# Loading x in four quarters, and splitting the first two weight units ahead of the first chunks of x

## The reference

```
f1 = swiglu(rms_norm(x, ffn1_pre_g), ffn1_w_gate, ffn1_w_up, ffn1_w_down)   # 1024 -> 2816 -> 1024
x  = x + 0.5 * rms_norm(f1, ffn1_post_g)
x  = x + rms_norm(token_mixer(rms_norm(x, mix_pre_g), ...), mix_post_g)      # 8 + 8 heads of 64
x  = x + 0.5 * rms_norm(swiglu(rms_norm(x, ffn2_pre_g), ...), ffn2_post_g)
gate = sigmoid(rms_norm(x, ple_pre_g) @ w_ple_gate)
x  = x + rms_norm(gate * (p @ w_ple_proj), ple_post_g)
```

## Time and profile before

| | |
|---|---|
| median of 3 runs | 1197.67 us (1196.76, 1197.9, 1197.67) |
| profiled execution, first to last instruction | 1196.8 us (no other time of it is shown) |
| TensorE matmuls busy | 1150.8 us, 96% |
| VectorE busy | 635.6 us, 53% |
| ScalarE busy | 510.1 us, 43% |
| GpSimd busy | 64.9 us, 5% |
| bytes read | 94.44 MB, 81 GB/s over the span |

### The profile page before, as it was taken

How to read it: one execution, slowest core, us unless ns; L and a number is a source line. 1 busy time by engine, 2 the same in 40 slices (tenths; PEclk the granted TensorE clock), 3 DMA queues, 4 the chain that set the end, 5 groups by cost and what they waited for, 6 DMA issues and landing times.

```text
span 1196.8 us, 15572 instructions
## 1 busy us (share of the span) xinstructions
PE 1150.8 (96%) x5066; PEld 938.9 (78%) x5066; DVE 635.6 (53%) x1007; ACT 510.1 (43%) x909; POOL 64.9 (5%) x68
## 2 busy tenths in 40 slices
PE   7999999999997999999999998799999999999897
PEld 6888888888885877888788776588888888888675
DVE  6454454542226865655556658945454454333745
ACT  5433333332224455646556653443333334333536
POOL 5000000000001300000000003400000000000120
PEclk9999999999998988998888899899999999999999
DMA  5233333322222311211111013133333334444001
GB/s 177 89 88 105 96 96 96 98 97 96 96 97 71 80 27 53 54 45 43 35 31 39 27 45 81 48 100 97 96 88 105 96 107 126 139 151 135 1 18 71
DMA packets 99011, 97.02 MB, mean 81 GB/s; under 512 B 7136, under 2 KB 82976, under 8 KB 98976
## 3 DMA queue, kind: packets, MB, share of 16 engines
q1 hardware_dynamic: 98976, 96.56, 27.1%
HBM read 94.44 MB, written 2.10 MB: 81 GB/s over the span
## 4 chain that ended last, share of the span: by engine, by line
PE 88%; DVE 7%; ACT 3%; issue 1%; DMA 0%; DVEq 0%; SPq 0%; ACTq 0%
PE bank L1106 28%; PE bank L1108 27%; PE bank L1107 27%; PE bank L1345 2%; DVE xT L788 2%; PE bank L1323 1%; DVE w_r L746 1%; DVE scratch L1052 1%; DVE xg L772 1%; PE bank L1311 1%; DVE acc L766 1%; ACT xg L459 1%; PE bank L1126 1%; PE bank L1376 1%; DVE scratch L1069 0%
## 5 line engine op out<-in xcount | busy, mean ns | idle before, releaser
L746 DVE TENSOR_TENSOR w_r<-w_raw,w_r 128x512 fp32r<-128x512 f32 x332 | 231.6, 706 | 386.1 <-ACT w_r L427 385.8
L427 ACT ACTIVATE w_r<-w_raw 128x512 fp32r<-128x512 f32 x332 | 206.2, 629 | 448.0 <-PE bank L1108 447.0
L1106 PE MATMUL bank<-xg,w_r 128*128 128x512 f32 x890 | 355.8, 400 | 4.6 <-DVE xg L772 4.6
L1107 PE MATMUL bank<-xg,w_r 128*128 128x512 f32 x890 | 351.5, 395 | 0.0
L1108 PE MATMUL bank<-xg,w_r 128*128 128x512 f32 x890 | 351.0, 394 | 0.0
L1106 PEld LDWEIGHTS bank<-xg,w_r 128*128 128x128 f32 x890 | 171.1, 192 | 42.5 <-DVE xg L772 6.9
L1108 PEld LDWEIGHTS bank<-xg,w_r 128*128 128x128 f32 x890 | 170.2, 191 | 36.4
L1107 PEld LDWEIGHTS bank<-xg,w_r 128*128 128x128 f32 x890 | 170.6, 192 | 35.6 <-issue 0.5
L1106 PE MATMUL bank<-big,w_r 128*128 (+1 forms) x416 | 164.2, 395 | 0.0
L1108 PE MATMUL bank<-big,w_r 128*128 (+1 forms) x416 | 162.9, 392 | 0.0
L1107 PE MATMUL bank<-big,w_r 128*128 (+1 forms) x416 | 162.9, 392 | 0.0
(11 more groups left out here) (165 smaller groups left out, 1086.5 us busy)
## 6 DMA issues: line engine op xcount, KB each, us to landing
w_raw<-in_ffn_w_gate SPq DMA_DIRECT2D x88, 256.0 KB, 2.8
w_raw<-in_ffn_w_up SPq DMA_DIRECT2D x88, 256.0 KB, 2.8
w_raw<-in_ffn_w_down SPq DMA_DIRECT2D x88, 256.0 KB, 2.6
w_raw<-in_w_in SPq DMA_DIRECT2D x36, 256.0 KB, 2.8
scratch<-in_w_ple_gate SPq DMA_DIRECT2D x16, 256.0 KB, 3.3
w_raw<-in_w_in SPq DMA_DIRECT2D x24, 128.0 KB, 2.2
scratch<-in_x SPq DMA_DIRECT2D x2, 1024.0 KB, 6.5
w_raw<-in_w_out SPq DMA_DIRECT2D x8, 256.0 KB, 2.7
```

Of the source, the lines that this page charges most:

```text
L427: act.activation(w_slot(0, slot, 0, 4 * P), w_raw[:, slot, :], ACT.Copy).then_inc(w_hi, 1)
L746: dve.tensor_tensor(w_slot(1, slot, 0, 4 * P), w_raw[:, slot, :], plain(w_slot(0, slot, 0, 4 * P)), SUB).then_inc(w_lo, 1)
L1106: pe.matmul(dst, w_hi_ap, m_hi, start=start, stop=False, skip_group_check=True)
L1107: pe.matmul(dst, w_lo_ap, m_hi, start=False, stop=False, skip_group_check=True)
```

## The change

SP loads x in four column quarters of 512 KB (two chunks each), in the order x0, unit 0, x1, unit 1, x2, x3, unit 2, unit 3. TensorE still transposes chunks 0 to 3 ahead of unit 0 and 4 to 7 behind it, with a wait per quarter. ScalarE gets a loop of its own, `prep_first`: the high part of unit 0 comes ahead of everything, that of unit 1 between the scaling and the squares of chunk 0, the others where they were. VectorE's loop is no longer staggered: copy k, then for k = 0 and 1 the low part of unit k, then the low part of chunk k, then for k = 2 and 3 the low part of unit k, then the units of `FIRST_AHEAD[k]`.

```diff
-            def load_x(half):
-                c = slice(512 * half, 512 * half + 512)
-                sp.dma_start(x_in[:, :, c], x_rows[:, :, c]).then_inc(x_loaded[half], 16)
+            def load_x(quarter):
+                c = slice(256 * quarter, 256 * quarter + 256)
+                sp.dma_start(x_in[:, :, c], x_rows[:, :, c]).then_inc(x_loaded[quarter], 16)
             load_x(0)
...
                     for j in range(SLOTS):
-                        if j == 2:
+                        step_unit(0, j)
+                        if j == 0:
                             load_x(1)
-                        step_unit(0, j)
+                        if j == 1:
+                            load_x(2)
+                            load_x(3)
...
+            def prep_first():
+                g = GAIN_AT["ffn1_pre_g"]
+                split_hi(0, 0)
+                for k in range(DC):
+                    act.wait_ge(x_ready, k + 1)
+                    act.activation(xg[:, 0, k, :], xT[:, k, :], ACT.Copy, scale=gains[:, g + k:g + k + 1]).then_inc(xg_hi, 1)
+                    if k == 0:
+                        split_hi(1, 1)
+                    squares(k, xT[:, k, :], par=k % 2)
+                    if 2 <= k < SLOTS:
+                        split_hi(k, k)
+                    for j in FIRST_AHEAD[k]:
+                        ahead(U_UP[0], 0, STEP_UNITS, j)
...
-            for k in range(DC + 1):
-                if k < DC:
-                    dve.wait_ge(x_t, k + 1)
-                    dve.tensor_copy(xT[:, k, :], bank[k][:, :]).then_inc(x_ready, 1)
-                if k:
-                    low(0, k - 1, "ffn1_pre_g")
-                    if k - 1 < SLOTS:
-                        lo_of(k, k - 1)
-                    for j in FIRST_AHEAD[k - 1]:
-                        ahead(U_UP[0], 0, STEP_UNITS, j)
+            for k in range(DC):
+                dve.wait_ge(x_t, k + 1)
+                dve.tensor_copy(xT[:, k, :], bank[k][:, :]).then_inc(x_ready, 1)
+                if k < 2:
+                    lo_of(k + 1, k)
+                low(0, k, "ffn1_pre_g")
+                if 2 <= k < SLOTS:
+                    lo_of(k + 1, k)
+                for j in FIRST_AHEAD[k]:
+                    ahead(U_UP[0], 0, STEP_UNITS, j)
...
-            def x_in_transpose(half):
+            def x_in_transpose(quarter):
-                pe.wait_ge(x_loaded[half], 16)
-                for k in range(4 * half, 4 * half + 4):
+                pe.wait_ge(x_loaded[quarter], 16)
+                for k in range(2 * quarter, 2 * quarter + 2):
...
                             if number == 0 and f == 0 and j == 0:
-                                x_in_transpose(1)
+                                x_in_transpose(2)
+                                x_in_transpose(3)
...
             x_in_transpose(0)
+            x_in_transpose(1)
             pe.wait_ge(const_hi, 1)
```

More of the change, by code:

```diff
@@ L184, in build @@
         first_gains_loaded = sem("first_gains_loaded")
-        x_loaded = [sem(f"x_loaded{i}") for i in range(2)]
+        x_loaded = [sem(f"x_loaded{i}") for i in range(4)]
         raw_loaded = [sem(f"raw_loaded{i}") for i in range(SLOTS)]
@@ L662, in early @@
                 return between
[L664 to L668, removed]
-                    ahead(U_UP[0], 0, STEP_UNITS, j)
-            prep(0, N_FFN1_PRE, "ffn1_pre_g", None, first_units)
+            prep_first()
             up(0, bank[7])
```

## The result

The changed kernel takes 1200.8 us (median of 15 runs), the kernel before 1197.9 beside it. The ratio is 1.0020 with a 95% interval of 1.0012 to 1.0028, so it is slower by 1.4 to 3.4 us. Executions of one kernel spread by more than that (1198.6 to 1202.4 for the changed one), so the small difference rests on the many runs. I had forecast +0.3 (1198.0, range 1195.2 to 1200.2). The profiled execution has a span of 1199.5 and a device time of 1201.62; the 2.1 us between the two are the same in every profiled run of the changed and the experimental kernels. So the kernel before's span of 1196.8 stands for about 1198.9, and not, as I wrote, for its fastest run.

A forecast was written before the change was run, and what follows sets the result against it. TensorE, busy 1150.8 of 1196.8 us, bounds the kernel. Early unit 0 (2.5) is lost to longer passes: sum at 34.86 against 34.78, or 34.5 by bookkeeping, taken as +0.3: 1197.67 + 0.3 = 1198.0, range 1195.2 to 1200.2.

The forecast's parts named there:

- Ahead of unit 1 lie the same 1.5 MB as before, so it stays at 7.98: Transfers at the start: unit 1 lands at 7.98 us as before, since the same bytes lie ahead of it.
- at 7.2: Transfers at the start: the second quarter of x lands at 7.2 us, behind unit 0 at 5.9.
- 34.86: End of unit 6 on TensorE: the last six matmuls end and the sum of squares comes at 34.86, before at 34.78.
- The rival with x not earlier: First transfers: a quarter lands late, first passes up to 1.3 later, sum 1.2 to 1.9 later, 1199.3 us; chance 0.08.
- The pass of 3.85 us: VectorE's new loop: 3.85 us per chunk instead of 2.3, or 3.11 without GpSimd's add in its way.
- The waits of TensorE: Unit 6: TensorE waits 0.7 us for its low part and 1.4 us for the low part of chunk 7.
- The head start of 2.5 us: Unit 0 on TensorE starts at 9.2 where it was 11.75, 2.5 us earlier.
- The order of the first splits: ScalarE splits unit 1 at 8.02, VectorE makes its low part at 9.07 to 9.75; copy 2 at 11.37, before 11.57.
- The clock of the first unit doesn't matter: Unit 0 on TensorE: if slow until 15.0, unit 1 starts at 16.4 and the waits in unit 6 take that up.
- No difference behind 36 us: Stretch behind the start: both kernels give TensorE the same work in the same order, so no difference arises there.
- The rival of a clock that falls in unit 6: TensorE's waits in unit 6 lower its clock, 12 to 16 matmuls take 0.2 more each: +3.1, 1200.8 us; chance 0.09.
- the 34.5 that I gave for the kernel before: Sum of squares in the kernel before by the forecast's own bookkeeping: 34.5, where the trace has 34.78.

The follow-up runs named there:

- e5: Changed kernel with GpSimd's first seven adds of the first norm cut to 8 of 512 columns: 1197.1 us, ratio 0.9992 to the kernel before.
- e4: Kernel before with only the changed loops of VectorE and ScalarE, x in halves and transfers as before: 1202.52 us, ratio 1.0032.
- e14: Changed kernel with quarters 0 and 1 of x both ahead of units 0 and 1: sum of squares at 37.04, time within 1200.6 to 1201.6 us.
- e2: Changed kernel with VectorE's loop staggered again, transfers and ScalarE as changed: 1199.56 us, ratio 1.0010 to the kernel before.
- e3: Kernel before with only the four quarters and their order, loops of VectorE and ScalarE as before: 1198.38 us, ratio 0.9998.
- e1_again: The changed kernel run again with no edit: 1201.12 us, ratio 1.0017 to the kernel before.
- e7: Changed kernel reordered: x0, units 0 and 1, then other quarters; unit 0 behind quarter 0 alone; VectorE staggered from chunk 2: 1196.62 us, ratio 0.9987 to kernel before.
- e12: The early-unit-0 version (x0, units 0 and 1 first) with the rest of x as one 1.5 MB transfer: 1195.99 us, ratio 0.9984 to kernel before.
- e6: Changed kernel, but SP waits for quarter 0 to land before it issues quarter 2: 1200.75 us, ratio 1.0018 to the kernel before.

## Why the prediction was wrong, by its own steps

**The step that failed: "Ahead of unit 1 lie the same 1.5 MB as before, so it stays at 7.98", and the second quarter "at 7.2".** They landed at 9.89 and 9.18. I took the bytes ahead of a transfer for its landing time, which in the kernel before held to 0.1 us in every row. Here quarter 1 was 0.3 to 2.1 us late in each of ten traces with x or other rows in this order. Its cost is plain in the chain, which begins with the landing of unit 1: copy 2 began at 12.99 instead of 11.37, 1.62 later, and the sum at 36.74 instead of 34.86, 1.88 later. From copy 2 to the sum it took 23.75 us, and I had 23.49. No trace of this order has unit 1 on time, so 34.86 itself was never tested; 26.8 to 27.0 us behind the 8.02 that I had for its high part would be 34.8 to 35.0, an estimate from the seven traces above. The rival with x not earlier had the sum 1.2 to 1.9 later and 1199.3, with a chance of 0.08. It comes nearest, but its step is another: there the first quarter is late, and here that one was on time. What makes a few parts late stays open.

**The pass of 3.85 us: right.** 3.84 measured, four times in a row, with the add's lock 0.7 of it (e5). The Trainium skill (SBUF — State Buffer, section "SBUF: two separate sides") gives the lock; the trace agrees, 1.40 us against the 0.69 of e5, and without the add the pass shrinks by 0.7. What I missed is how often they meet: in e4 and e14 the low parts of unit 1 and of chunk 1 both met an add.

**The waits of TensorE: right in place and size.** In unit 6 two matmuls stand 0.83 and 1.48 us behind the ones before them, where 0.23 is usual: waits of 0.6 and 1.25, forecast as 0.7 and 1.4. Unit 1 began at 17.61, right behind copy 3 (done at 17.51).

**The head start of 2.5 us: wrong, 0.9.** Unit 0 began at 10.83, straight behind the transposes of quarter 1, which could start only at 9.21. The copy of chunk 1 was there since 9.17, as forecast (9.15).

**The order of the first splits: costed at nothing beside the rest, wrong.** ScalarE splits unit 1 ahead of the squares of chunk 0 and of scaling chunk 1, and VectorE makes unit 1's low part ahead of that of chunk 1. With unit 1 at 9.89 both engines stand until 9.94 and 10.60. e2 against e3 gives the price with unit 1 at 9.1 and 9.2: 34.22 - 32.46 = 1.76. With unit 1 on time it needn't be harmless either: in e4, with the same loops, copy 2 began at 13.69, where I expected 12.6 and the kernel before has 11.57.

So the loss at the start divides into three, from one kernel to the next: the quarters -2.32, the early splits +1.76, the loop in one row +1.75 (34.22 to 35.97). They sum to +1.19 for e1_again; the first trace has 0.8 more, from a quarter that was 0.8 later still. The parts hold in this order alone: the same loops cost 2.68 with x in halves (e4), and 3.51 here.

**"The clock of the first unit doesn't matter": right for the changed kernel, wrong for all that keep the head start.** **No difference behind 36 us: not borne out by the traces.** The first one loses another 0.7 there (2.7 of the span less 1.96), which is within what one trace differs from the next (last section). The rival of a clock that falls in unit 6 didn't happen: the matmuls behind it stand 0.23 apart. That its 1200.8 is the measured median is luck.

**The range.** 1200.8 lies 0.6 above its end. Of the difference, the start gave 1.96 in the trace and the stretch behind 0.7; the range had a late x at 1199.3 and nothing for the stretch behind. Two smaller slips changed nothing: the 34.5 that I gave for the kernel before isn't worked out (2.72 a unit and 0.45 from 18.02 give 34.79, so my sum was +0.1, not +0.3), and the 2 us of fixed cost stand in the same page of the Trainium skill (DMA: Bandwidth & Descriptors) under "Anatomy of one DMA — SWDGE (gpsimd) path", fitted to transfers that GpSimd issues, where SP issues these.

## What to carry to other kernels

A loop in which two engines hand each chunk to each other should keep one chunk between them; putting the steps of one chunk in a row made each pass 1.5 us longer here, and cost 1.75 us in the end. Work that waits for a transfer should not stand ahead of work that doesn't on the same engine: it turned a late landing into a late start of everything, microsecond for microsecond. And a landing forecast from the bytes ahead is a lower bound, which wants a case for being late where the order of transfers is new.

## What the runs showed of the hardware that I had not expected

The same work behind the sum takes 1160.8 to 1163.8 us, from one trace to the next. TensorE's stretch from 656 to 716 us shows it (busy time, instructions, granted clock, DMA share, GB/s). First e3 (0.88, as in the kernel before), then e7:

```profile
656.00:716.00 60.00, 57.09 (x259) 0.88 0.11 36
```

```profile
656.00:716.00 60.00, 57.13 (x271) 0.93 0.12 36
```

The mean granted clock is 0.93 in e5, e7 and e12, which all have 1160.8 or 1160.9 behind the sum, and 0.85 to 0.88 in the kernel before, the changed one, e1 to e4 and e6 (1162.0 to 1163.8). 12 more matmuls fit into the same 60 us.

It isn't set by when the sum starts: e3 starts it at 32.46 and takes 1163.8, e5 and e7 at 32.08 and 32.60 and take 1160.8. And it isn't a property of a kernel. The twelve executions of e7 take 1195.4 to 1196.0 us where the mean granted clock of the whole run is 0.956 (six of them), 1197.2 and 1197.4 at 0.955, and 1198.2 to 1198.6 at 0.953 (four), with no edit between them. The traces of e5, e7 and e12 all come from executions at 0.956, and about half of the other executions of these kernels ran at less. What decides which one an execution gets wasn't tried. So the stretch behind the sum can't be compared by one trace of each kernel, and what a gain at the start is worth in the end is known only within the intervals: -1.3 to +0.8 us for the 2.3 of e3, -2.6 to -0.5 and -3.0 to -0.7 for the 2.2 and 2.1 of e7 and e12.
